# Chunk products of a delta-rule mixer spread over the four quarters of TensorE's array, with an upper-triangular solve reordered, in a two-layer decoder trunk

## The chip, the cores and the metric

The kernel runs on one core of one Trainium2 chip. The metric is the device time of one execution in microseconds (us). Three runs of the kernel before are shown; their median is 1519.89 us, from 1516.77 to 1520.2 us.

## What is computed

Two layers of a decoder trunk on 512 tokens of 1024 channels, all in fp32: a first layer whose mixer is half a gated linear recurrence (Griffin) and half an RWKV-7 time mix, a second layer whose mixer is retention, and after each mixer an MLP with squared ReLU. What the change touches is the recurrence of the RWKV-7 time mix, for 8 heads of 64 channels:

```python
def step(s, inp):
    r_t, w_t, k_t, v_t, z_t, bb_t = inp
    sz = jnp.einsum("bhij,bhj->bhi", s, z_t)
    s = s * w_t[:, :, None, :] + sz[..., None] * bb_t[:, :, None, :] + v_t[..., None] * k_t[:, :, None, :]
    return s, jnp.einsum("bhij,bhj->bhi", s, r_t)
...
_, y = lax.scan(step, s0, (tm(r_h), tm(w_h), tm(k_h), tm(v_h), tm(z_h), tm(b_h)))
```

Run token by token this would be 512 dependent steps. The kernel cuts the tokens into 8 chunks of 64 and does all that lies within a chunk by 64x64 matrix products, so that only 8 steps from chunk to chunk depend on each other.

## The kernel before, in words

The 8 heads go in 4 pairs (`PAIRS`), two heads of 64 channels over the 128 partitions. For each pair p the program runs `front_*` (projections of the pair, its vectors, and the normalising and output projection of pair p-1) and then `chunks_*`; after the last pair, `front_*` once more for the last output. Each engine has its own hand-written list of instructions (`_pe`, `_act`, `_dve`, `_pool`), and they meet only at semaphores: `need(...)` waits for names of this pair, `was(...)` for names of the pair before. After these stages come MLP, retention and MLP, which the change doesn't touch.

`chunks_pe` is the stage in question. A matrix of it is a tile of 128x512: partitions 0 to 63 hold one head, 64 to 127 the other, and every 64 columns are a chunk, so it holds 16 squares of 64x64. `by_chunk` (line 725) multiplies two such tiles square by square: 16 matmuls of 64x64 into one PSUM bank, each head's on its own rows and its own columns of the array. `ROWS` are the two halves of the partitions. There are 28 such products per pair. Four of them only turn a vector tile by multiplying with a unit matrix (`z_turned`, `v_turned`, `k_turned`, `b_turned`); the others make the chunk's triangular matrices (`azb`, `azk`, `ark`, `arb`), powers of the part on the 16-wide diagonal blocks (`m2`, `m4`, `m8`) and the inverse built from them (`e2`, `e4`, `e8` into `dt`), the rest of the inverse (`po`, `po2`, `sol`), and what the chunk-to-chunk steps need (`w1`, `w2`, `gg`, `qq`). Almost every result goes from PSUM to SBUF before it is used again, either by an ACT copy (`evac`, line 1002) or by a DVE operation (`masked` line 1196, `copied` 1200, `add` 1192, and line 1231).

```python
for c in range(NCH):
    cols = slice(c * C, (c + 1) * C)
    for rows in ROWS:
        mm = pe.matmul(bank[b][rows, cols], lhsT[rows, cols], rhs[rows, :] if rhs is eye2 else rhs[rows, cols],
                       start=True, stop=True)
```

The second part of `chunks_pe` is the loop over the 8 chunks (lines 902 to 919). For chunk c it first issues the products that need no state (902, 903 for the state, 907, 908 for the output), then waits for the state of the chunk before (`state`, a DVE multiplication at line 1238), adds the state's own product (915) into the same PSUM region, and the output's (919). `y_heads` ends it, and ACT's copy `ys` (938) and the next pair's `low_ranks` (783, 784) follow.

Weights stream through a ring of three buffers (`RING`): SP loads 1 MB, ACT rounds it (`split_hi`, 297), DVE takes the rest (`split_lo`, 303, 2.28 us for a full one), and PE waits in `chunk_ready`. Some of these splits stand inside `chunks_act` and `chunks_dve`. The pairs 1 and 2 (`FILLED`) have done the linear recurrence's last steps (`lru_drive`, `lru_scan`, `ya_out`, `ya_low`) in the front; pairs 0 and 3 do them on DVE in the chunk stage.

## Time and profile before

| | |
|---|---|
| runs, median (lowest to highest) | 1519.89 us (1516.77 to 1520.2) |
| the profiled execution, its own time | 1520.04 us |
| its span, first to last instruction | 1518.3 us |
| PE, PEld busy | 1475.6, 1232.3 us |
| DVE, ACT, POOL busy | 831.6, 504.0, 73.5 us |
| granted TensorE clock, mean | 0.986 |
| `by_chunk` matmul records, 4 pairs | 3584 |

The profiled execution lies 0.15 us from the median of the runs. PE is a matmul row of the profile, PEld a weight load. An fp32 matmul leaves two records of each kind, so that one `by_chunk` product of 16 matmuls leaves 32. A row's duration is from its first instruction's start to its last one's end; matmuls are pipelined, so the time from the start of one group to the start of the next is the rate.

### The profile page before, as it was taken

What the parts mean: (1) busy time and instruction counts of PE and PEld (TensorE: products, weight loads), DVE (VectorE), ACT (ScalarE), POOL (GpSimd) and SP (SyncE); (2) the same over time, 40 slices, a digit from 0 to 9 for tenths busy, and PEclk for the clock granted to TensorE, in tenths of its full rate; (3) what the DMA queues carried; (4) which work ended last, traced back from release to release, by engine and by line L of the source; (5) the groups of instructions that cost most, each with busy time, mean ns of one, the idle gap of its engine ahead of it and who ended that gap; (6) DMA issues with size and microseconds to landing.
All of it is one profiled execution on the core that took longest, in us unless ns stands there. A gap on an engine that the chain in (4) does not pass through costs nothing.

```text
span 1518.3 us, 23219 instructions
## 1 busy us (share of the span) xinstructions
PE 1475.6 (97%) x10404; PEld 1232.3 (81%) x10404; DVE 831.6 (55%) x1035; ACT 504.0 (33%) x578; POOL 73.5 (5%) x67
## 2 busy tenths in 40 slices
PE   7999999998999999999899999999998999999998
PEld 5888878786888888888788888888887888888886
DVE  7767585757644445363675455454447635354455
ACT  7444443534322222122343332332434313122222
POOL 1000000002100000000300000000003000000000
PEclk9999999998999999999899999999998999999999
DMA  4202020201322222223032213132131332222322
GB/s 180 71 8 98 3 89 18 84 4 56 125 95 100 92 102 90 105 88 107 28 111 84 83 58 109 57 104 91 56 111 42 112 110 83 93 102 90 105 88 79
DMA packets 19731, 125.62 MB, mean 83 GB/s; under 512 B 2288, under 2 KB 2288, under 8 KB 5808
## 3 DMA queue, kind: packets, MB, share of 16 engines
q1 hardware_dynamic: 19088, 121.23, 23.3%
q0 software_dynamic: 544, 2.91, 0.6%
q8 instruction: 82, 1.34, 0.4%
q14 instruction: 17, 0.14, 0.0%
HBM read 122.03 MB, written 2.10 MB: 82 GB/s over the span
## 4 chain that ended last, share of the span: by engine, by line
PE 88%; DVE 5%; ACT 3%; DMA 1%; POOL 1%; issue 1%; SPq 0%; DVEq 0%; POOLq 0%
PE bank L330 19%; PE bank L336 18%; PE bank L333 18%; PE bank L725 7%; PE bank L534 4%; PE bank L531 4%; PE bank L535 4%; PE bank L1331 2%; PE bank L1334 2%; PE bank L1328 2%; PE bank L344 2%; DVE XL L423 1%; DMA raw<-weights 1%; ACT WH L297 1%; POOL h L462 1%
## 5 line engine op out<-in xcount | busy, mean ns | idle before, releaser
L330 PE MATMUL bank<-XH,WH 128*128 128x512 f32 x944 | 381.6, 404 | 24.6 <-DVE XL L423 12.6
L333 PE MATMUL bank<-XL,WH 128*128 128x512 f32 x944 | 372.0, 394 | 0.0
L336 PE MATMUL bank<-XH,WL 128*128 128x512 f32 x944 | 371.8, 394 | 0.0
L303 DVE TENSOR_TENSOR WL<-raw,WH 128x2048 fp32r<-128x2048 f32 (+1 forms) x111 | 249.8, 2251 | 175.6 <-ACT WH L297 175.5
L297 ACT ACTIVATE WH<-raw 128x2048 fp32r<-128x2048 f32 (+1 forms) x111 | 208.4, 1877 | 277.7 <-DMA raw<-weights 277.7
L330 PEld LDWEIGHTS bank<-XH,WH 128*128 128x128 f32 x944 | 180.3, 191 | 66.6 <-issue 28.7
L333 PEld LDWEIGHTS bank<-XL,WH 128*128 128x128 f32 x944 | 180.5, 191 | 38.7 <-issue 2.6
L336 PEld LDWEIGHTS bank<-XH,WL 128*128 128x128 f32 x944 | 179.9, 191 | 38.9
L647 ACT ACTIVATE AH<-relu 128x512 fp32r<-128x512 f32 x64 | 40.5, 633 | 249.7 <-DVE relu L672 249.7
L330 PE MATMUL bank<-AH,WH 128*128 128x512 f32 x256 | 99.7, 389 | 0.1
L672 DVE SCALAR_TENSOR_TENSOR relu<-bank,rB 128x512 f32<-128x512 f32 x64 | 44.1, 690 | 101.3 <-PE bank L336 101.3
L333 PE MATMUL bank<-AL,WH 128*128 128x512 f32 x256 | 99.6, 389 | 0.0
L531 PE MATMUL bank<-WH,AH 128*128 128x512 f32 x256 | 99.6, 389 | 0.0
L534 PE MATMUL bank<-WL,AH 128*128 128x512 f32 x256 | 99.6, 389 | 0.0
L336 PE MATMUL bank<-AH,WL 128*128 128x512 f32 x256 | 99.6, 389 | 0.0
L535 PE MATMUL bank<-WH,AL 128*128 128x512 f32 x256 | 99.6, 389 | 0.0
L494 DVE TENSOR_TENSOR f<-f,bank 128x512 f32<-128x512 f32 x64 | 43.3, 686 | 90.8 <-PE bank L336 90.6
L725 PE MATMUL bank<-W,W 64*64 64x64 f32 x1920 | 63.2, 219 | 4.1 <-DVE W L1192 3.8
L725 PEld LDWEIGHTS bank<-W,W 64*64 64x64 f32 x1920 | 59.5, 135 | 6.9 <-issue 6.3
L330 PEld LDWEIGHTS bank<-AH,WH 128*128 128x128 f32 x256 | 48.0, 188 | 10.4 <-DVE AL L679 0.5
L531 PEld LDWEIGHTS bank<-WH,AH 128*128 128x128 f32 x256 | 48.0, 188 | 10.0
L333 PEld LDWEIGHTS bank<-AL,WH 128*128 128x128 f32 x256 | 48.0, 188 | 10.0
(298 smaller groups left out, 2054.3 us busy)
## 6 DMA issues: line engine op xcount, KB each, us to landing
raw<-weights SPq DMA_DIRECT2D x107, 1024.0 KB, 4.8
raw<-weights SPq DMA_DIRECT2D x8, 512.0 KB, 5.0
h<-x_fm SPq DMA_DIRECT2D x4, 512.0 KB, 8.0
out_tm<-hT SPq DMA_DIRECT2D x8, 256.0 KB, 2.1
rc<-ret_const POOLq DMA_DIRECT2D x1, 1536.0 KB, 6.8
pp<-pairs POOLq DMA_DIRECT2D x4, 199.0 KB, 5.1
cst<-const SPq DMA_DIRECT2D x1, 577.0 KB, 11.9
gain_row<-last_gain POOLq DMA_DIRECT2D x1, 512.0 KB, 3.5
```

The costliest lines, as they stand in the source:

```text
L297: nc.scalar.activation(WH[i][:, :n], raw[i][:, :n], ACT.Copy).then_inc(S("w_hi"), 1)
L303: nc.vector.tensor_tensor(WL[i][:, :n], raw[i][:, :n], WH[i][:, :n], ALU.subtract).then_inc(S("w_lo"), 1)
L330: mm = pe.matmul(bank[b][:], wh, xh, start=(k == 0), stop=False)
L333: mm = pe.matmul(bank[b][:], wh, xl, start=False, stop=False)
L336: mm = pe.matmul(bank[b][:], wl, xh, start=False, stop=(k == len(xs) - 1))
L494: nc.vector.tensor_tensor(f[:, m, :], f[:, m, :], bank[b][:], ALU.add).then_inc(S(f"acc_free{b}"), 1)
L531: mm = pe.matmul(bank[b][:], AH[:, kt, tok], wh, start=(kt == 0), stop=False)
L534: pe.matmul(bank[b][:], AH[:, kt, tok], wl, start=False, stop=False)
L535: mm = pe.matmul(bank[b][:], AL[:, kt, tok], wh, start=False, stop=(kt == KT - 1))
L647: nc.scalar.activation(AH[:, j, :], relu[:, j % 2, :], ACT.Square).then_inc(S("a_hi"), 1)
L672: nc.vector.scalar_tensor_tensor(relu[:, j % 2, :], bank[b][:], 0.0, rB[:], ALU.max, ALU.mult).then_inc(S(f"acc_free{b}"), 1)
L725: mm = pe.matmul(bank[b][rows, cols], lhsT[rows, cols], rhs[rows, :] if rhs is eye2 else rhs[rows, cols], start=True, stop=True)
```

## The change

It rewrites the chunk stage on all engines. Nothing outside `chunks_*` changes but two things: the copy `ys` reads another layout, and `front_dve` of pair 1 has one more `split_lo`.

1. Two neighbouring PSUM banks become a "twin" (`bank[2 * pr + j]`). A product of kind `vectors_to_t` or `turned` reads head j from rows j of the array and writes the result of chunk (i, par) to partitions `ROWS[par]` of bank 2·pr+j: its 16 matmuls use all four combinations of row half and column half. The matrices change layout with each such product (head on the partitions, or chunk parity on them). `kept` and `vectors_to_n` stay on the two diagonal quarters as before.
2. `two_vectors_to_t` and `two_turned`: two products with the same left factor become 16 matmuls of 64x128, the right factors side by side (azb_t with arb_t, azk_t with ark_t, e2 with m4_t, yz with yx).
3. `by_token`: the four turns become four 128x128 transpositions each.
4. `sol_t` goes; instead of one matrix for the solution, `t1z`, `t1x` and `ip2` are formed. The chunk's own products are 26: 13 on four quarters, 4 doubled on four quarters, 5 on two quarters, 4 of transpositions.
5. In the loop over chunks, the products without state move into `over_tokens`; they sum over tokens, which now lie on rows `ROWS[par]`, while the state's products sum over channels on rows of each head. Both add into the same PSUM region, and PE waits for its own semaphore `over_tokens` between them.
6. DVE and ACT lists are reordered. For pairs 0 and 3 `split_lo(4p+4)` moves from the middle of `chunks_dve` to its end; for pair 0 `split_lo(5)` moves to the front of pair 1.

```diff
-        def by_chunk(pe, b, lhsT, rhs, signal, left=0):
...
+        CH = [(i, par, j) for i in range(NCH // 2) for par in range(2) for j in range(2)]
...
+        def two_sums(pr, j, par, i):
+            return bank[2 * pr + j][ROWS[par], :].rearrange("p (w x) -> p w x", w=2)[:, :, i * C:(i + 1) * C]
...
+        def two_turned(pe, pr, lhsT, rhs, signal):
+            for i, par, j in CH:
+                rows, cols = ROWS[j], square(par, i)
+                mm = pe.matmul(two_sums(pr, j, par, i), lhsT[rows, cols], rhs[rows, :, cols], start=True, stop=True)
+            mm.then_inc(S(signal), 1)
...
+        def by_token(pe, b, vector, signal):
+            for i in range(NCH // 2):
+                mm = pe.transpose(bank[b][:, i * P:(i + 1) * P], vector[:, i * P:(i + 1) * P], eye)
+            mm.then_inc(S(signal), 1)
...
+        def turned(pe, pr, lhsT, rhs, signal):
+            for i, par, j in CH:
+                rows, cols = ROWS[j], square(par, i)
+                mm = pe.matmul(bank[2 * pr + j][ROWS[par], i * C:(i + 1) * C], lhsT[rows, cols], rhs[rows, cols],
+                               start=True, stop=True)
+            mm.then_inc(S(signal), 1)
...
+            vectors_to_t(pe, 3, W[5], W[6], "azb", 1)
+            need("lru_i", "rd_ready")
+            two_vectors_to_t(pe, 2, W[6], z_r, "azb_t")
+            pe.wait_ge(S("acc_free1"), use.now(1))
+            vectors_to_n(pe, 1, W[6], W[5], "azb_n")
+            need("nn", "nt", "g_out", "lru_r")
+            turned(pe, 1, W[0], W[1], "m2")
+            need("o")
+            turned(pe, 3, W[1], W[0], "m2_t")
+            need("nt_n")
+            by_token(pe, 1, W[5], "z_turned")
+            need("m2_s", "m2_ts")
+            turned(pe, 1, W[10], W[9], "m4")
+            need("e1")
+            two_turned(pe, 3, W[9], unit_squared, "e2")
...
+            need("m8_i", "e4_s")
+            turned(pe, 1, W[9], W[5], "e8")
...
+            need("w1_s", "b_by_token")
+            turned(pe, 1, W[7], Bt, "gg")
+            turned(pe, 2, W[7], lax, "qq")
...
+            for c in range(1, NCH):
+                i, par = c // 2, c % 2
+                prev = slice((c - 1) * C, c * C)
+                pe.wait_ge(S("over_tokens"), NCH * p + c + 1)
+                pe.wait_ge(S("state"), (NCH - 1) * p + c)
...
+                if c < NCH - 1:
+                    pe.wait_ge(S("over_tokens"), NCH * p + c + 1)
+                    over_tokens(c + 1)
...
+            if p == 1:
+                split_lo(dve, 4 * p + 1)
             split_lo(dve, 4 * p + 2)
...
+            if p not in FILLED:
+                split_lo(dve, 4 * p + 4)
+            if p:
+                split_lo(dve, 4 * p + 5)
```

What this does to the instructions' order, at three places. First PE at the start of pair 0's chunk stage. Names are tiles with their numbers (W0 to W11 are work tiles; `z_r` holds z and the decayed r side by side, `unit_squared` the unit-added matrix beside m2's turned form); a trailing x16 counts equal instructions. Before:

```order
L725 MATMUL bank5<-W5_67,W6_68 64x64 x16
L725 MATMUL bank6<-W6_68,W5_67 64x64 x16
L725 MATMUL bank7<-cst,W5_67 64x64 x16
L725 MATMUL bank2<-cst,W2_64 64x64 x16
L725 MATMUL bank3<-W1_63,W0_62 64x64 x16
L725 MATMUL bank4<-W0_62,W1_63 64x64 x16
L725 MATMUL bank7<-W5_67,W7_69 64x64 x16
L725 MATMUL bank2<-Rd_88,W7_69 64x64 x16
```

Now (a twin is printed by its first bank, so bank0 is bank 1 here):

```order
L744 MATMUL bank6<-W6_66,z_r_72 64x64 x16
L758 MATMUL bank4<-z_r_72,W6_66 64x2x64 x16
L777 MATMUL bank0<-z_r_72,W6_66 64x64 x16
L783 MATMUL bank2<-W1_63,W0_62 64x64 x16
L783 MATMUL bank6<-W0_62,W1_63 64x64 x16
L771 MATMUL bank0<-cst,z_r_72 128x128 x4
L783 MATMUL bank2<-W9_69,unit_squared_71 64x64 x16
L764 MATMUL bank6<-unit_squared_71,W9_69 64x2x64 x16
```

The turns of z and v, which stood as the third and fourth product and gave DVE time for its masks, are now four transpositions further on; m2 stands as the fourth product.

Second, PE in the loop over chunks, one round of pair 0. Before:

```order
L915 MATMUL bank4<-W3_65,W11_73 64x64 x2
L919 MATMUL bank2<-W10_72,W3_65 64x64 x2
L902 MATMUL bank3<-W9_71,Bt_79 64x64
L903 MATMUL bank3<-Vt_81,Kt_80 64x64
L902 MATMUL bank3<-W9_71,Bt_79 64x64
L903 MATMUL bank3<-Vt_81,Kt_80 64x64
L907 MATMUL bank2<-ARB_82,W9_71 64x64
```

Now:

```order
L1011 MATMUL bank2<-W3_65,W11_70 64x64 x2
L1015 MATMUL bank6<-unit_squared_71,W3_65 64x64 x2
L989 MATMUL bank0<-W9_69,Bt_78 64x64
L990 MATMUL bank0<-Vt_80,Kt_79 64x64
L989 MATMUL bank0<-W9_69,Bt_78 64x64
L990 MATMUL bank0<-Vt_80,Kt_79 64x64
L996 MATMUL bank6<-lax_89,W9_69 64x64
```

The instructions and their order are the same; what is new is which rows of the array they use and the wait on PE's own `over_tokens` ahead of 1011.

Third, DVE at the end of the last pair's chunk stage and in the front after it. Before:

```order
L1238 TENSOR_SCALAR W_65<-bank,PC 128x64 x7
L303 TENSOR_TENSOR WL_57<-raw_56,WH_58 128x2048
L494 TENSOR_TENSOR f<-f,bank 128x512
L1067 SCALAR_TENSOR_TENSOR Vt<-bank,Zt 128x512
L494 TENSOR_TENSOR f<-f,bank 128x512 x2
```

Now (line 1352 is the state's multiplication, 312 the split, 503 the addition to f, 1179 the centring of y):

```order
L1352 TENSOR_SCALAR W_65<-bank,PC 128x64 x7
L312 TENSOR_TENSOR WL_54<-raw_53,WH_55 128x2048
L312 TENSOR_TENSOR WL_57<-raw_56,WH_58 128x2048
L503 TENSOR_TENSOR f<-f,bank 128x512
L1179 SCALAR_TENSOR_TENSOR Vt<-bank,z_x 128x512
```

A second split of weights stands between the last state and the centring of y.

## Rows read from the trace of the kernel before

**Rows 1.** The page: busy time by engine, and the chain by line

```profile
PE 1475.6 (97%) x10404; PEld 1232.3 (81%) x10404; DVE 831.6 (55%) x1035; ACT 504.0 (33%) x578; POOL 73.5 (5%) x67
...
PE 88%; DVE 5%; ACT 3%; DMA 1%; POOL 1%; issue 1%; SPq 0%; DVEq 0%; POOLq 0%
PE bank L330 19%; PE bank L336 18%; PE bank L333 18%; PE bank L725 7%; PE bank L534 4%; PE bank L531 4%; PE bank L535 4%; PE bank L1331 2%; PE bank L1334 2%; PE bank L1328 2%; PE bank L344 2%; DVE XL L423 1%; DMA raw<-weights 1%; ACT WH L297 1%; POOL h L462 1%
```

**Rows 2.** Busy time by stretch: the chunk products, then pair 0's loop

```profile
core 0: us, PE busy (x) PEld busy (x) DVE busy (x) ACT busy (x) POOL busy (x), PEclk, DMA share, GB/s
61.67:89.59 27.92, 26.97 (x897) 26.65 (x897) 17.46 (x23) 13.11 (x17) 2.54 (x2) 1.00 0.08 22
89.59:95.53 5.94, 5.75 (x180) 5.45 (x175) 2.90 (x9) 0.00 (x0) 0.00 (x0) 1.00 0.03 6
144.06:171.90 27.84, 26.89 (x897) 26.58 (x897) 13.84 (x18) 8.96 (x13) 2.53 (x2) 1.00 0.07 23
```

**Rows 3.** Timeline, PE (start, us, engine, line, operation, tiles, count)

```profile
25.48 0.60 PE L350 MATMUL bank<-cst,small 128*128 128x128 f32 x4
25.84 0.48 PE L330 MATMUL bank<-XH,WH 128*128 128x512 f32 x1
...
47.16 1.02 PE L830 MATMUL bank<-W,cst 128*128 128x512 f32 x2
48.02 1.02 PE L832 MATMUL bank<-gate_in,pp 128*128 128x512 f32 x2
...
104.38 1.09 PE L740 MATMUL bank<-cst,lninv 128*64 128x128 f32 x16
105.40 0.50 PE L330 MATMUL bank<-XH,WH 128*128 128x512 f32 x1
```

**Rows 4.** Timeline, PE and its weight loads at pair 0's first products

```profile
61.12 0.39 PE L333 MATMUL bank<-XL,WH 128*128 128x512 f32 x1
61.35 0.39 PE L336 MATMUL bank<-XH,WL 128*128 128x512 f32 x1
61.67 2.08 PE L725 MATMUL bank<-W,W 64*64 64x64 f32 x64
63.58 2.03 PE L725 MATMUL bank<-cst,W 64*64 64x64 f32 x64
...
61.66 0.14 PEld L725 LDWEIGHTS bank<-W,W 64*64 64x64 f32 x2 [0.35 <-issue]
```

**Rows 5.** Timeline, all engines, from sol_t to w1 and its copy

```profile
83.59 1.23 PE L725 MATMUL bank<-W,W 64*64 64x64 f32 x32
...
84.94 0.69 DVE L1192 TENSOR_TENSOR W<-W,bank 128x512 f32<-128x512 f32 x1 [0.54 <-PE bank L725]
...
85.78 2.08 PE L725 MATMUL bank<-W,W 64*64 64x64 f32 x64 [0.95 <-DVE W L1192]
86.96 0.60 ACT L1002 ACTIVATE W<-bank 128x512 f32<-128x512 f32 x1 [4.52 <-PE bank L725]
```

**Rows 6.** Timeline, DVE: at the stage's entry, pair 0, then pair 1

```profile
61.77 0.69 DVE L718 TENSOR_TENSOR Uag<-bank,rB 128x512 f32<-128x512 f32 x1 [3.60 <-PE bank L336]
62.50 0.69 DVE L1155 SCALAR_TENSOR_TENSOR Kt<-ARB,Kt 128x512 f32<-128x512 f32 x1
63.11 1.38 DVE L1196 TENSOR_TENSOR W<-bank,cst 128x512 f32<-128x512 f32 x2
64.41 0.68 DVE L1196 TENSOR_TENSOR O<-bank,cst 128x512 f32<-128x512 f32 x1
...
144.17 0.69 DVE L492 COPY f<-bank 128x512 f32<-128x512 f32 x1 [0.67 <-PE bank L336]
```

**Rows 7.** Timeline, pair 0's loop: PE, then DVE

```profile
90.92 0.33 PE L915 MATMUL bank<-W,W 64*64 64x64 f32 x4 [0.19 <-DVE W L1238]
...
91.17 0.33 PE L902 MATMUL bank<-W,Bt 64*64 64x64 f32 x4
...
91.64 0.33 PE L915 MATMUL bank<-W,W 64*64 64x64 f32 x4
...
89.89 0.69 DVE L1192 TENSOR_TENSOR W<-Rd,bank 128x512 f32<-128x512 f32 x1 [0.31 <-PE bank L725]
90.50 0.28 DVE L1238 TENSOR_SCALAR W<-bank,PC 128x64 f32<-128x64 f32 x1
```

**Rows 8.** Timeline around the last pair's end: DVE, then PE

```profile
332.27 2.28 DVE L303 TENSOR_TENSOR WL<-raw,WH 128x2048 fp32r<-128x2048 f32 x1
...
335.30 0.69 DVE L1067 SCALAR_TENSOR_TENSOR Vt<-bank,Zt 128x512 f32<-128x512 f32 x1
...
337.78 0.95 PE L733 MATMUL bank<-cst,ARK 128*128 128x2 f32 x8
```

**Rows 9.** Timeline, DVE in pair 1's front

```profile
112.13 0.69 DVE L718 TENSOR_TENSOR Ur<-bank,rB 128x512 f32<-128x512 f32 x1 [0.18 <-PE bank L336]
...
133.23 0.69 DVE L718 TENSOR_TENSOR Uag<-bank,rB 128x512 f32<-128x512 f32 x1 [3.61 <-PE bank L336]
```

More of the change, by code:

```diff
@@ new lines, in turned, with kept @@
+        def turned(pe, pr, lhsT, rhs, signal):
+            for i, par, j in CH:
+                rows, cols = ROWS[j], square(par, i)
+                mm = pe.matmul(bank[2 * pr + j][ROWS[par], i * C:(i + 1) * C], lhsT[rows, cols], rhs[rows, cols],
+                               start=True, stop=True)
+            mm.then_inc(S(signal), 1)
+        def kept(pe, b, lhsT, rhs, signal):
+            for i, par, j in CH:
+                rows, cols = ROWS[j], square(par, i)
+                mm = pe.matmul(bank[b][rows, cols], lhsT[rows, cols], rhs[rows, cols], start=True, stop=True)
+            mm.then_inc(S(signal), 1)
@@ new lines, in chunks_pe, with over_tokens @@
+            turned(pe, 2, W[7], lax, "qq")
+            need("w2_s", "k_by_token")
+            def over_tokens(c):
+                i, par = c // 2, c % 2
+                rows = ROWS[par]
+                for j in range(2):
+                    cols = square(j, i)
+                    if c < NCH - 1:
+                        to = bank[1 + par][ROWS[j], i * C:(i + 1) * C]
+                        pe.matmul(to, Bt[rows, cols], W[9][rows, cols], start=True, stop=False)
+                        mm = pe.matmul(to, Kt[rows, cols], Vt[rows, cols], start=False, stop=(c == 0))
+                if c == 0:
+                    mm.then_inc(S("state_full"), 1)
+                for j in range(2):
+                    cols = square(j, i)
+                    to = bank[6 + par][ROWS[j], i * C:(i + 1) * C]
+                    pe.matmul(to, W[9][rows, cols], lax[rows, cols], start=True, stop=False)
+                    mm = pe.matmul(to, Vt[rows, cols], ARK[rows, cols], start=False, stop=(c == 0))
+                mm.then_inc(S("over_tokens"), 1)
@@ L899, in chunks_pe @@
+            over_tokens(0)
+            need("g_s")
+            over_tokens(1)
+            need("q_s")
+            for c in range(1, NCH):
+                i, par = c // 2, c % 2
                 prev = slice((c - 1) * C, c * C)
+                pe.wait_ge(S("over_tokens"), NCH * p + c + 1)
+                pe.wait_ge(S("state"), (NCH - 1) * p + c)
                 if c < NCH - 1:
                     for rows in ROWS:
-                        pe.matmul(bank[3 + c % 2][rows, cols], Bt[rows, cols], W[9][rows, cols], start=True, stop=False)
@@ L1222, in chunks_dve @@
[L1222 to L1233 removed]
+            need("po2")
@@ L1249, in front_pool @@
+            pool.wait_ge(*nth("nt_n", p + 1))
+            nc.gpsimd.tensor_tensor(chunked(W[4]), chunked(W[4]), table(K_EYE2), ALU.add).then_inc(S("e1"), 1)
         def front_pool(pool, p):
```

276 lines of the change are left out of this document (138 added, 138 removed).

## The prediction

> **What bounds the kernel now.** I read the page first: PE is busy for 97% of the span and holds 88% of the chain that ended last; DVE is at 55%, ACT at 33% [rows 1]. The program is bound by PE nearly everywhere, so a change pays by what it takes from PE's path. `by_chunk` (L725) alone is 7% of that chain, some 105 us. The table by stretch shows the stage the same way: of the 27.92 us of pair 0's chunk products PE is busy 26.97, and pair 1's stretch is 27.84 us long; then comes the loop with 5.94 us [rows 2]. Four pairs make some 135 us in which the change can act.
>
> **What a product costs now.** Two products run from 61.67 to the next group at 63.58 [rows 4]; over the stage the spacing is 0.933 us for 32 records, 29 ns each (the last of a row's records still needs 0.22 us: 64 records, 2.08 us, are 1.86 + 0.22). What is that 29 ns? A full-width fp32 product of 512 columns takes 48.02 - 47.16 = 0.86 us for two records, 0.43 each [rows 3], so 64 columns should take 0.43/8 = 54 ns. The stage runs twice as fast: the two heads' diagonal quarters work at the same time. The spread at L740 tells of the other direction: 16 records of 128 columns, each 107 ns by the same scale, would take 1.72 us one by one and take 105.40 - 104.38 = 1.02 [rows 3]. There both matmuls use all 128 rows and differ in the column half. So row halves overlap and column halves overlap; both at once, with four quarters, stands nowhere in the trace.
>
> **The change, part by part.**
>
> *Products on four quarters.* 13 single ones. Bounds: 0.933 us (no denser than the trace shows) and half of it, 0.467, if four overlap as two do now. I take 0.467, since either direction alone is shown to overlap fully. The 4 doubled ones: 32 records of 107 to 110 ns over four quarters, 0.88 us; if only two overlap, 1.76.
>
> *The rest of PE's list.* 5 products stay on two quarters, 5 x 0.933 = 4.67. 4 turns of four 128x128 transpositions: L350 has the same four, 0.60 us less the 0.16 that its last one needs beyond its slot, 0.44 each [rows 3], 1.76. They leave the 64x64 shape eight times per pair: at 61.35 the next start would have come 0.23 us later, at 61.58, and came at 61.67, with PEld idle for 0.35 [rows 4]. I take 0.09 a switch, 0.72; bounds 0 and 0.35. Sum: 13 x 0.467 + 4 x 0.88 + 4.67 + 1.76 + 0.72 = 16.7 us, against 28 x 0.933 = 26.1 now.
>
> *What PE will wait for.* With PE faster, the path product, copy, product matters. Its pieces: sol_t's first record at 83.59, DVE at 84.94, w1 on PE at 85.78: after DVE's end (85.63) 0.15 us; PE's last record ends 0.05 to 0.12 before the copy starts [rows 5]. An ACT copy is 0.60 us long, a DVE one 0.69, and DVE starts the next 0.61 to 0.65 later (63.11 to 64.41 for two); I take 0.61 [rows 5, 6]. I wrote the four new lists down against each other with these durations. For pair 0 five waits remain: m2 waits 0.60 for nt (DVE is busy with L718 and L1155 until 63.11, 1.44 after the stage's start [rows 6]), m4 0.46 for DVE's copy of m2_t, e8 0.42 for e4's copy, gg 0.49 for w1's, the turn of z 0.14. PE ends at 18.8 us after the start. In pairs 1 and 2 DVE is free 0.7 after the start (144.17 + 0.69 [rows 6]) and PE ends at 18.3; pair 3 enters like pair 0. The same writing-out gives 27.56 for the kernel before, 0.36 less than the 27.92 measured, so I add 0.36: 19.15 and 18.65. Gain: 2 x (27.92 - 19.15) + 2 x (27.84 - 18.65) = 35.9 us.
>
> *The loop.* Now the state's path sets it: L915 at 90.92, again at 91.64, 0.72 a round [rows 7]; PE's 24 records would need 0.70, so both are near. After the change PE issues state and output products (8 records, 0.23), `over_tokens` (16 records on two column halves of one row half, 0.47), then waits until the last of these is complete (0.16 more) and for the semaphore (0.06 to 0.10): 0.94 a round. The state's path (0.72) hides under that. Six rounds x 0.2 = 1.2 a pair, **4.8 us lost** in four. Bounds: 0 (if the state's path covers it) and 0.4 a round, 10 us.
>
> *The splits of weights.* Each is 2.28 us on DVE. In pair 3 a second one now lies between the last state and `head_centred` (L1067) [rows 8]. Before: split at 332.27, centring at 335.30, its square on ACT, and PE's sums at 337.78 without a wait. Now two splits end 4.56 after 332.27, then L494 and L1067 (0.61 + 0.07 + 0.69), ACT 0.63 and 0.1: 6.7 after, where PE arrives 5.5 after. PE waits **1.1 us**, once. In pair 1's front a further split comes after `kkinv`; L718 at 112.13 had waited for PE and moves 2.2 later. Queued behind it are the mixes, the convolution and `split_lo(7)`; DVE idles 3.61 us before 133.23 [rows 9], which takes it up. Cost 0; without that cover, 2.2. Pair 0's own split now ends where the next one ended before; PE's k projection may wait 0.2. SP's loads move earlier with the stage and have nothing to wait for.
>
> *Sum.* 35.9 - 4.8 - 1.1 - 0.2 = 29.8 us. From the profiled execution's 1520.04 that is **1490.2 us**; its distance of 0.15 from the median of the runs is nothing beside this.
>
> **The rivals.**
>
> *A. Starts come no closer than now.* The densest stretch of the trace is 29 ns a matmul record, each with its weight load [rows 2, 4]; issue or weight loading may be what sets it, and four quarters then change nothing for 64 columns. The doubled products would still pay. All 22 products but the turns cost 0.933: PE's list 20.5 + 1.76 + 0.72 = 23.0, with 0.9 of waits and the 0.36 24.3, a gain of 3.6 x 4 = 14.4, less 6.1: **1511.7 us**. For it: two row halves at 54 ns give 27, close to 29, and any other limit near there would look the same. Against: L740's spacing, also twice the single rate, is at 64 ns, so that 29 fits the columns and no fixed floor is needed to explain either. The Trainium skill ("TensorE: Matmul & The Clock Gate", Part 1, on the 56 ns) has such a floor at about 25 ns from start to start, whatever the columns; by that a single product would be 0.80 and a doubled one stays 0.88, and the estimate would be 1505. No row here shows a floor.
>
> *B. The copies set the stage.* DVE gets 18 operations of the stage and ACT 15, now with four-dimensional patterns over two banks. At the 0.61 spacing DVE needs 11.0 us and in pair 0 another 3.0 for the recurrence: under PE's 16.7. If the patterns make each copy half as long again (0.92 and 0.74), the lists end 4.8 later in pair 0 and 3.7 in pair 1, 17 in all: **1507 us**. For it: no row shows such a pattern. Against: L1196 reads a broadcast table in three dimensions and is as long (0.68) as a plain L718 (0.69) [rows 6]. The skill ("TensorEngine Tiling (Array Packing)", PSUM Bottleneck) says that after a fourfold speedup the copies may become the bound; the rows don't show that here.
>
> *C. Column halves on the same row half don't overlap for 64-row tiles.* Then single ones stay 0.933 and doubled ones 1.76; PE's list is 25.6 + 0.72 and the stage 27.6, a gain of 0.3 a pair. In the loop `over_tokens` uses one row half only and takes 0.93 instead of 0.47: with six rounds 2.8 more a pair. Sum: -1.4 + 11.3 + 4.8 + 1.3 = 16.0: **1536 us**, slower. It decides as soon as four records of 64 columns take 0.11 us, and not 0.06. For it: one row half has to feed two different streams, which no row shows (in L740 both take the unit matrix). Against: in L740 two matmuls of different column halves do overlap.
>
> **How the numbers follow.** The forecast has 0.60, A 0.17, B 0.09, C 0.10; 0.04 is for the rest. The forecast's own range: switches free and the loop at its old rate give 1482; the loop at 0.4 a round, switches at 0.35 (8 us more) give 1503. A and B reach to 1512. To leave no more than 2 in 10 out, the range goes from 1484 to 1512; C is outside. Within 0.3% (1515.5 to 1524.6, about what a measurement of this kernel can tell from no change) lies only a mixture, A with a dearer loop, or C with half its overlap: 0.05. Faster 0.85, slower 0.10.
>
> **What would show it.** In the profile after: `turned` rows (L783) of 16 matmuls every 0.47 us when nothing is waited for (0.8 to 0.93 is A, over 0.93 for doubled ones, L758 and L764, is C); `over_tokens` groups with L1011 every 0.94 us; transpositions (L771) at 0.44; copies at 0.60 and 0.69 (B otherwise); the chunk products about 19 us long per pair, the loop 7 us; DVE's idle time in the stage shrinking to a few us; an idle stretch of about 1 us on PE ahead of the head sums after the last pair. PE's granted clock should stay at 2.4 GHz through the stage, 1.00 in the stretches now [rows 2]: should the waits bring it to the lower level, the forecast is wrong by more than its terms. The forecast is wrong in its main term if the four quarters give less than 6 us a pair.

## The result, and the profile after

| | before | changed |
|---|---|---|
| runs on one chip, median (lowest to highest) | 1519.18 us (1516.77 to 1520.2) | 1494.09 us (1493.28 to 1496.79) |
| ratio, 95% interval | 1 | 0.9849 (0.9835 to 0.9863) |
| the profiled execution, its span | 1518.3 us | 1495.0 us |
| PE, PEld records | 10404 each | 9700 each |

The change is faster by 25 us, where 29.8 were forecast; 1494.1 lies in the range, 3.9 us above the number. The page of the changed kernel answers to [rows 1]:

```profile
PE 1445.6 (97%) x9700; PEld 1194.6 (80%) x9700; DVE 831.3 (56%) x1039; ACT 509.9 (34%) x590; POOL 73.2 (5%) x67
...
q8 instruction: 77, 1.26, 0.3%
...
PE 89%; DVE 5%; ACT 3%; issue 1%; POOL 1%; DMA 1%; SPq 0%; DVEq 0%; ACTq 0%; POOLq 0%
```

PE is still the bound. The line in the middle is a DMA queue (packets, MB, share) that the prediction passed over. It brings instructions, 1.26 MB in 77 packets of 16 KB. The 19400 records of PE and PEld are 252 to a packet. It is taken up again below.

Busy time by stretch of the changed kernel: pair 0's chunk products and its loop, then the chunk products of pairs 1, 2 and 3. Columns as in [rows 2].

```profile
63.15:83.42 20.27, 18.71 (x722) 16.88 (x721) 14.94 (x23) 12.00 (x19) 2.52 (x2) 1.00 0.09 30
83.42:90.85 7.43, 6.86 (x185) 5.95 (x176) 3.23 (x10) 2.56 (x2) 0.00 (x0) 1.00 0.01 2
139.52:159.08 19.56, 18.59 (x721) 17.09 (x720) 13.31 (x19) 9.76 (x16) 2.51 (x2) 1.00 0.09 30
215.55:236.99 21.44, 18.68 (x721) 17.01 (x721) 13.57 (x19) 9.69 (x16) 2.49 (x2) 1.00 0.09 29
282.04:303.75 21.71, 18.91 (x721) 16.94 (x721) 14.89 (x23) 11.99 (x19) 2.51 (x2) 1.00 0.16 52
```

The four chunk stretches are 82.98 us together. Before they were 27.92, 27.84, 28.40 and 28.37, together 112.53: 29.55 us are gained, not 35.9. The four loops, first start to last start, are 7.42, 7.78, 7.31 and 7.31 where they were 5.79 each: 6.7 lost. Two things lie outside. Pair 0's stage starts at 63.15 and not at 61.67, since PE's granted clock was at 1.2 GHz for most of the 4 us in the row below (of the changed kernel, 0.57 for the mean), and what follows pair 3 is 1.84 us shorter. In that last part, up to PE's last record, the clock was at the lower level for 37.5 us before and for 34.1 us in the changed kernel; by half of the difference, an estimate, up to 1.7 of the 1.84 are the clock's and not the change's. -29.55 + 6.7 + 1.48 - 1.84 is -23.2; the spans differ by 23.3.

```profile
23.50:27.50 4.00, 4.00 (x14) 3.17 (x13) 0.78 (x1) 1.26 (x1) 0.00 (x0) 0.57 0.00 0
```

That early fall of the clock was in some profiled executions of the kernels below and not in others with the same program up to there. It belongs to the execution, not to the change; the other three runs of the changed kernel are 2 to 3.5 us shorter than the profiled one.

Timeline of the changed kernel, PE at pair 0's first products (as [rows 4]):

```profile
63.15 0.69 PE L744 MATMUL bank<-W,z_r 64*64 64x64 f32 x32
63.66 1.05 PE L758 MATMUL bank<-z_r,W 64*64 64x128 f32 x32
64.54 1.11 PE L777 MATMUL bank<-z_r,W 64*64 64x64 f32 x32
65.97 1.25 PE L783 MATMUL bank<-W,W 64*64 64x64 f32 x64 [0.32 <-DVE W L1306]
67.15 0.66 PE L771 MATMUL bank<-cst,z_r 128*128 128x128 f32 x4
68.12 0.69 PE L783 MATMUL bank<-W,unit_squared 64*64 64x64 f32 x32 [0.32 <-DVE unit_squared L1314]
68.61 1.08 PE L764 MATMUL bank<-unit_squared,W 64*64 64x128 f32 x32
69.48 1.08 PE L758 MATMUL bank<-z_r,W 64*64 64x128 f32 x32
```

A single product on four quarters takes 0.49 us to the next start (68.12 to 68.61; its row of 0.69 less the last record's 0.22 is 0.47), where one took 0.93. A doubled one takes 0.87 (68.61 to 69.48). The waits for DVE's mask and for its copy of m2_t are there. The copies have their old lengths: timeline of the changed kernel, one of ACT and one of DVE.

```profile
66.72 0.60 ACT L1101 ACTIVATE W<-bank 128x512 f32<-128x512 f32 x1 [1.39 <-PE bank L783]
...
67.28 0.69 DVE L1314 COPY unit_squared<-bank 128x512 f32<-128x512 f32 x1 [0.22 <-PE bank L783]
```

So A (no closer starts), B (longer copies) and C (column halves don't overlap) all fall by the rows that were to decide. What then stretches the stage? The same view for pair 3, where two products break in their middle:

```profile
287.51 0.86 PE L764 MATMUL bank<-unit_squared,W 64*64 64x128 f32 x22
289.07 0.48 PE L764 MATMUL bank<-unit_squared,W 64*64 64x128 f32 x9 [0.70 <-issue]
...
295.10 0.62 PE L764 MATMUL bank<-z_x,W 64*64 64x128 f32 x16
296.64 0.67 PE L764 MATMUL bank<-z_x,W 64*64 64x128 f32 x16 [0.92 <-issue]
```

Nothing is waited for between two matmuls of one product, and yet PE and its weight loads stand still. "issue" names no releaser. In start-to-start time the long gaps are 0.54 us in pair 0, 0.55 in pair 1, 1.34 and 1.04 in pair 2, 0.97 and 1.19 in pair 3. Pair 1's is the only one that costs next to nothing: it lies in w2's product, and the wait ahead of gg, 0.47 us in pair 0, is not there. Laid beside the instruction queue's packets, each gap ends 1.24 to 1.55 us after one of them has arrived:

```
pair   packet arrived   PE goes on
0      72.72            74.27
1      156.50           157.94
2      218.82           220.33
2      224.04           225.28
3      287.65           289.07
3      295.21           296.64
```

That gave **theory S**: PE's instructions come in blocks of 256, one in 3.4 us or more. A product has 64 of them (16 matmuls, two passes each, each with its load). Two-quarter products at 0.93 us use a block in 3.73 us, which the queue keeps up with (the kernel before has one such stop, 0.47 us from start to start at 305.23, in pair 3); four-quarter ones at 0.47 us use it in 1.9. The Trainium skill ("Runtime: NRT & Kernel Launch", Instruction fetch mechanics) has the queue, the 16 KiB block of 256 instructions and that the next block is fetched while the current one runs; the trace agrees. It also says that this is hidden. The rows above say that here it is not.

The traces hold a sharper sign of S than the packets. Count every instruction of PE from the program's start, the matmul records, the weight loads and the few semaphore instructions among them, and divide by 256. In the traces of the two kernels and of the twelve experiments below there are 94 places inside a product of 64x64 tiles where PE stood idle for over 0.15 us and the profile names no releaser. All 94 have the remainder 193 or 194, whatever the product, the pair or the kernel; waits and tiles would spread them over all 256 remainders. What the stops share is their place in the count.

### The profile page after: what moved, and what is told of

Same layout as the page of the kernel before. It is cut to its first block, busy times and chain, and to the rows that moved or that the text cites. A ratio compares the mean times of both kernels' runs of the same rounds, so it can differ in the third digit from the quotient of the medians.

```text
span 1495.0 us, 21859 instructions
## 1 busy us (share of the span) xinstructions
PE 1445.6 (97%) x9700; PEld 1194.6 (80%) x9700; DVE 831.3 (56%) x1039; ACT 509.9 (34%) x590; POOL 73.2 (5%) x67
## 3 DMA queue, kind: packets, MB, share of 16 engines
q8 instruction: 77, 1.26, 0.3%
## 4 chain that ended last, share of the span: by engine, by line
PE 89%; DVE 5%; ACT 3%; issue 1%; POOL 1%; DMA 1%; SPq 0%; DVEq 0%; ACTq 0%; POOLq 0%
PE bank L339 20%; PE bank L345 20%; PE bank L342 19%; PE bank L543 4%; PE bank L540 4%; PE bank L544 4%; PE bank L1450 2%; PE bank L1447 2%; PE bank L1444 2%; PE bank L783 2%; PE bank L353 1%; PE bank L790 1%; DVE WL L312 1%; DVE XL L432 1%; POOL h L471 1%
## 5 line engine op out<-in xcount | busy, mean ns | idle before, releaser
L544 PEld LDWEIGHTS bank<-WH,AL 128*128 128x128 f32 x256 | 48.1, 188 | 10.0
L345 PEld LDWEIGHTS bank<-AH,WL 128*128 128x128 f32 x256 | 48.0, 188 | 9.9
```

Of the source, the lines that this page charges most:

```text
L345: mm = pe.matmul(bank[b][:], wl, xh, start=False, stop=(k == len(xs) - 1))
L544: mm = pe.matmul(bank[b][:], AL[:, kt, tok], wh, start=False, stop=(kt == KT - 1))
```

## The experiments

Theories beside S: **O**, the gaps belong to the stage's own order and waits; **F**, a least distance from start to start; **W**, the loop is set by PE's wait for its own `over_tokens`.

**1. The products without state two chunks ahead.** Three banks for the state and four for the output, so that `over_tokens(c + 2)` is issued where `over_tokens(c + 1)` was, and no wait for PE's own products is needed.

```diff
-                if c < NCH - 1:
-                    pe.wait_ge(S("over_tokens"), NCH * p + c + 1)
-                    over_tokens(c + 1)
+                if c < NCH - 2:
+                    over_tokens(c + 2)
```

> The products without state are issued two chunks ahead (chunk c+2 after the state's product of c), with three PSUM banks for the states and four for the outputs, so that PE's wait for its own over_tokens is met long before; the copy ys becomes three copies. Theory W (PE's wait for its own completion is what made a round 0.97 to 1.02 us in the changed kernel, against 0.72 before): rounds fall to 0.72 to 0.75, 1.5 us a pair; the longer copy at the end and the later third group give back some 0.6, so about 1490.5 us. Rival B (a round is dear because of the row halves that over_tokens uses: two column halves on one row half don't overlap fully): rounds stay near 1.0 and the time is 1494 to 1497.

Ratio 0.9831 (0.9816 to 0.9845), 1492.04 us. Timeline of this kernel, PE in pair 0's loop (L1015 is the state's product, L1011 in the changed kernel):

```profile
84.18 0.33 PE L1015 MATMUL bank<-W,W 64*64 64x64 f32 x4
...
85.78 0.33 PE L1015 MATMUL bank<-W,W 64*64 64x64 f32 x4
```

Two rounds in 1.60, 0.80 a round, where the changed kernel has 0.97 and 1.02 in turn; 0.72 to 0.75 had been expected. The four loops are 6.58, 6.63, 6.79 and 6.55 us: 3.3 less. In the changed kernel the wait is visible too (instructions of L1011, what ended PE's idle time before them):

```profile
L1011 PE MATMUL bank<-W,W x96: 218/228/267, 84.8 to 310.3; 64*64 64x64 f32 x96
...
  PE bank L997: 3.9, 20
```

W holds for 3.3 of the 6.7 us lost. Of the rest some 2 us (0.08 a round, 24 rounds) are that a round's 24 records on the new layout need 0.80 and not 0.72. That is not rival B: four neighbouring records still start in 0.12 us, and what is added lies where the next state product follows on `over_tokens` (0.20 in its place). By the totals alone the two kernels are not apart (the intervals overlap); by the rounds they are.

**2. Without doubling.** Each doubled product as two single ones, 256 instructions more a pair, the same columns.

```diff
-            for i, par, j in CH:
...
-                mm = pe.matmul(two_sums(pr, j, par, i), lhsT[rows, cols], rhs[rows, :, cols], start=True, stop=True)
+            for w in range(2):
+                for i, par, j in CH:
...
+                    mm = pe.matmul(two_sums(pr, j, par, i)[:, w, :], lhsT[rows, cols], rhs[rows, w, cols], start=True,
+                                   stop=True)
```

> Each of the 4 doubled products becomes two single ones of 16 matmuls with 64 columns, on the same four quarters, with the same left factors: PE gets 256 more instructions per pair (64 x 4) and nearly the same array time (0.93 for 0.88 us). Theory O (array time and waits for copies explain the stage): 0.2 us a pair, 1495 us. Theory S (PE's instructions come in 16 KB blocks of 256, and on four quarters it uses them up faster than the next block is ready, some 3.5 us each): up to 3.5 us more a pair, 1500 to 1508 us, with idle stretches of 0.5 to 1.5 us inside products that begin shortly after a block's packet has ended.

Ratio 0.9957 (0.9943 to 0.9971). The chunk stretches of this kernel, columns as before:

```profile
61.67:84.67 23.00, 19.39 (x850) 17.57 (x849) 15.04 (x23) 12.05 (x19) 2.52 (x2) 1.00 0.10 27
140.83:164.92 24.09, 20.66 (x850) 18.86 (x849) 13.32 (x19) 9.84 (x16) 2.50 (x2) 0.93 0.08 25
```

All four are 96.5 us, 13.5 more than in the changed kernel. Pair 0 has the clock at 1.00 throughout and is longer by 2.7 us, for 256 instructions at the same array time. In pairs 1, 2 and 3 the clock fell as well (0.93 each, 0.07 of 24 us, 1.7 us a pair at most): 5.1 of the 13.5. The other 8.4 are S's, 2.1 a pair, less than the 3.4 of a full block. In pair 0 the stops account for all of it: 0.68, 1.57 and 0.94 us, 2.65 more than the changed kernel's 0.54. The total, 1512.6 us by the ratio, is longer than the 1500 to 1508 that S had said, by about what the clock took, which S had not.

**3 and 4. The order of the 16 matmuls.** The same matmuls, in another order: one quarter after the other, and one column half after the other.

```diff
-        CH = [(i, par, j) for i in range(NCH // 2) for par in range(2) for j in range(2)]
+        CH = [(i, par, j) for j in range(2) for par in range(2) for i in range(NCH // 2)]
```

```diff
-        CH = [(i, par, j) for i in range(NCH // 2) for par in range(2) for j in range(2)]
+        CH = [(i, par, j) for par in range(2) for i in range(NCH // 2) for j in range(2)]
```

> The same matmuls on the same quarters, but quarter by quarter: four neighbours in the list use one quarter, then four the next. If each quarter has a queue deep enough for its four (16 instructions), a product still takes 0.47 us and the time is 1494. If PE looks only a few instructions ahead, the quarters work one after the other: a single product then takes 32 x 0.058 = 1.87 us and a doubled one 3.5, some 28 us a pair more, 1600 us. Anything between tells how far it looks.

> The order of the matmuls keeps to one column half for eight neighbours (both row halves in turn), then the other. This prices the use of four quarters at once. If only what stands next to each other overlaps, single products take 0.93 us and doubled ones 1.76, and the stage is 27.6 us a pair, as in rival C of the prediction: 1494 + 4 x 6.8 = 1521 us. With a deep look-ahead it stays at 1494.

Ratios 1.0227 (1.0212 to 1.0242) and 0.9896 (0.9881 to 0.9911). Pair 0's chunk stretch and, from the timeline, m2 with m2_t (two single products), first by quarter:

```profile
61.50:96.30 34.80, 34.26 (x716) 33.07 (x716) 15.82 (x23) 13.42 (x20) 2.53 (x2) 1.00 0.05 18
```

```profile
66.42 2.46 PE L783 MATMUL bank<-W,W 64*64 64x64 f32 x61
```

The same two of the kernel by column half:

```profile
61.52:83.75 22.23, 21.56 (x715) 20.28 (x716) 14.97 (x23) 12.24 (x19) 2.50 (x2) 1.00 0.09 28
```

```profile
64.54 1.56 PE L783 MATMUL bank<-W,W 64*64 64x64 f32 x64
```

61 records in 2.24 us are 37 ns each, against 15 in the changed kernel. The 37 ns lie between these 15 and the 54 of one quarter alone, the estimate of the prediction. So the quarters work fully side by side only where neighbours in the program lie on different ones; four successive matmuls on one quarter let the fifth overtake them only in part. Both totals, 1553.7 and 1503.4 us by the ratios, lie between the values that had been expected (1494 and 1600; 1494 and 1521). All four pairs by quarter take 34.83 us, alike to 0.01: a slow array has no gaps, as S says. By column half a single product takes 0.67 (64 records in 1.34), the stretches are 22.23 us in three pairs and 23.21 in the last, and only that one has a gap inside a product (0.48).

**5. The turns as fp32 products.** Two passes each, 32 instructions more a pair.

```diff
-                mm = pe.transpose(bank[b][:, i * P:(i + 1) * P], vector[:, i * P:(i + 1) * P], eye)
+                mm = pe.matmul(bank[b][:, i * P:(i + 1) * P], vector[:, i * P:(i + 1) * P], eye, start=True, stop=True)
```

> The four turns per pair are four matmuls with the unit matrix again, full 128 rows, instead of transpositions: the same 128 columns, but fp32 products leave two records each where a transposition leaves one. Theory S (PE's instruction supply, blocks of 256 instructions some 3.5 us apart, is what stretches the chunk stage of the changed kernel): each turn 0.44 us longer on the array (1.76 a pair, four turns) and 32 instructions more per pair (0.43 us of supply); 1499 to 1501 us, with a turn (L771) of 0.87 us from start to next start. Rival T (the turns lie under waits and cost nothing; their form is indifferent): 1493 to 1495.

Ratio 0.9893 (0.9872 to 0.9914), 1501.26 us. Timeline of this kernel, PE, z's turn in pair 1:

```profile
143.30 1.16 PE L771 MATMUL bank<-cst,z_r 128*128 128x128 f32 x8
144.39 0.69 PE L783 MATMUL bank<-W,unit_squared 64*64 64x64 f32 x32
```

A turn takes 1.09 to the next start; in the changed kernel z's takes 0.97 in pair 0, of which a wait of 0.32, which is gone here. The chunk stretches are 85.9 us, 2.9 more, not 7, and the loops are 1.2 longer: between T and S, since two turns lie under a wait (the idle time of 0.32 us behind z's and of 0.28 behind v's in the changed kernel are both gone here). By the ratio the kernel is 6.7 us slower, so only some 4 of it are found here, and I take nothing more from it.

**6. Half a block at the start.** 32 small matmuls (128 instructions) ahead of all; the stage is untouched.

```diff
+            for _ in range(32):
+                pe.matmul(bank[7][0:C, 0:C], vec[0:C, 0:C], vec[0:C, 0:C], start=True, stop=True)
```

> 32 small fp32 matmuls (64 columns, 128 instructions, half a block of 256) are issued once at the program's start into a bank that nobody reads; the chunk stage is that of the changed kernel, instruction for instruction. Theory S: the ends of the blocks fall at other places of the stage, so the long gaps move: the chunk products of the four pairs are no longer 20.3, 19.6, 21.4, 21.7 us but another set between 19.3 and 22, in which at least two pairs differ by over 0.5 us from before, and the gaps stand at other products; the total stays within 2.5 us of 1494. Rival O (the gaps belong to the stage's own order, tiles and waits): the same four durations to 0.2 us, gaps at the same products; the total 1494 to 1495.

Ratio 0.9872 (0.9854 to 0.9891). Chunk stretches of this kernel:

```profile
61.45:84.36 22.91, 19.04 (x722) 17.07 (x723) 14.94 (x23) 12.00 (x19) 2.51 (x2) 1.00 0.08 27
140.37:162.47 22.10, 19.23 (x722) 17.06 (x722) 13.79 (x19) 9.88 (x16) 2.51 (x2) 1.00 0.09 27
218.39:238.58 20.19, 18.77 (x721) 16.88 (x721) 13.48 (x19) 9.57 (x16) 2.50 (x2) 1.00 0.09 30
283.70:303.14 19.44, 18.26 (x721) 16.67 (x721) 14.83 (x23) 12.12 (x19) 2.51 (x2) 1.00 0.18 59
```

The same instructions take 22.9, 22.1, 20.2, 19.4 us, not 20.3, 19.6, 21.4, 21.7. Pair 3 has lost both long gaps, pair 0 has three (0.77, 1.05, 1.53). O falls. S's sizes were too narrow: two stretches are over 22 us, and by the ratio the kernel is 3.5 us slower than the changed one, not 2.5 at most.

**7. A whole block at the start.** The same with 64 matmuls.

```diff
+            for _ in range(64):
+                pe.matmul(bank[7][0:C, 0:C], vec[0:C, 0:C], vec[0:C, 0:C], start=True, stop=True)
```

> 64 small fp32 matmuls at the program's start, 256 instructions: a whole block, where the earlier run had half a one. Theory S: the ends of the blocks come back to where they are in the changed kernel, and with them the gaps: chunk products of about 20.3, 19.6, 21.4, 21.7 us (each within 0.5 us, since the arrival of a block also varies by itself), with the long gaps inside e2's product and inside yz's in pair 3; total 1494 to 1499 us (the small matmuls themselves cost what they did in the run with 32, up to 4 us). Rival V (the lengths vary from run to run and the number of instructions has no part in it): another set of lengths, as different from the changed kernel's as that of the run with 32.

Ratio 0.9877 (0.986 to 0.9893). First and last chunk stretch of this kernel:

```profile
66.63:87.18 20.55, 18.84 (x722) 17.06 (x722) 14.82 (x23) 11.99 (x19) 2.51 (x2) 1.00 0.10 30
...
285.48:306.67 21.19, 18.90 (x721) 16.93 (x721) 14.89 (x23) 11.98 (x19) 2.51 (x2) 1.00 0.15 53
```

20.55, 19.72, 20.50, 21.19: the changed kernel's set again, pair 2 a little outside the half microsecond (0.94). The gaps of pair 3 stand in e2's and yz's products, 6.1 and 13.2 us after its start (6.1 and 13.4 in the changed kernel). The place is set by the number of instructions ahead, the size also by when the block happens to arrive. The total, 1500.5 us by the ratio, lies 1.5 above the expected range. Experiments 1 and 11 have as many instructions ahead of pair 3 as the changed kernel, and their gaps stand in the same two products there (0.70 and 1.19 us; 0.98 and 1.19). V falls.

**8. The supply by itself.** 16 more products ahead of azb in pairs 1, 2 and 3, which nobody waits for.

```diff
+            for _ in range(16 if p else 0):
+                for i, par, j in CH:
+                    rows, c0 = ROWS[j], (2 * i + par) * C
+                    n = {1: C, 2: 16, 3: C}[p]
+                    out = bank[6 + j][ROWS[j if p == 3 else par], i * C:i * C + n]
+                    pe.matmul(out, W[5][rows, c0:c0 + C], W[6][rows, c0:c0 + n], start=True, stop=True)
```

> Ahead of azb, in pairs 1, 2 and 3, stand 16 more products of 16 matmuls each (1024 instructions, four blocks of 256), with nothing to wait for and nobody waiting for them. Pair 1: 64 columns on four quarters, the form of azb itself. Pair 2: the same with 16 columns. Pair 3: 64 columns on the two diagonal quarters. Theory S (the supply of instructions, a block of 256 every 3.4 us): pairs 1 and 2 take alike, 10 to 14 us, whatever the columns, in dense bursts with gaps of over 0.3 us between them; pair 3 takes the array's own 16 x 0.933 = 15 us with no gap. Rival F (a least distance from start to start of 25 to 27 ns a record): pairs 1 and 2 take 13 to 14 us at an even pace, with no gap. Rival R (no such limit; the gaps of the chunk stage come from its waits): pair 1 takes 16 x 0.467 = 7.5 us, pair 2 less than that. The whole kernel is longer by about the sum of the three stretches, less 1 to 2 us of waits that they cover.

This kernel was run once; all that is read from it lies within that one trace. Its timeline, PE: four quarters with 64 columns, four quarters with 16, two quarters with 64. L744 is azb, where each stream ends.

```profile
139.41 4.19 PE L935 MATMUL bank<-W,z_r 64*64 64x64 f32 x270
144.75 2.10 PE L935 MATMUL bank<-W,z_r 64*64 64x64 f32 x128 [1.15 <-issue]
148.75 1.90 PE L935 MATMUL bank<-W,z_r 64*64 64x64 f32 x113 [1.91 <-issue]
150.44 0.23 PE L744 MATMUL bank<-W,z_r 64*64 64x64 f32 x3
...
235.91 2.51 PE L935 MATMUL bank<-W,z_r 64*64 64x16 f32 x157
239.69 2.05 PE L935 MATMUL bank<-W,z_r 64*64 64x16 f32 x128 [1.27 <-issue]
243.69 6.58 PE L935 MATMUL bank<-W,z_r 64*64 64x16 f32 x226 [1.95 <-issue]
250.01 0.35 PE L744 MATMUL bank<-W,z_r 64*64 64x64 f32 x2
...
317.63 15.08 PE L935 MATMUL bank<-W,z_r 64*64 64x64 f32 x509
332.50 0.27 PE L744 MATMUL bank<-W,z_r 64*64 64x64 f32 x1
```

The first 270 records (540 instructions, two blocks and a little) run at 14.7 ns each, then PE stands for 1.15 us. Then come 128 records, which with their 128 loads are exactly a block, and again a gap. From block to block it is 4.00 us (144.75 to 148.75; 239.69 to 243.69). With 16 columns the gaps are the same and so is the pace inside a block, 14.4 to 14.7 ns. The stream on two quarters takes 14.87 us with no gap, 29 ns a record. S holds; F and R fall. Two points went otherwise. A starved block takes 4.0 us and not 3.4, although a stream that uses one in 3.72 us is not starved at all. And in pair 2 the granted clock fell from 2.4 to 1.2 GHz during the stream, in the second gap, so that its 14.1 us can't be set against pair 1's 11.03. A starved stream is thus slower per product (4.00/4 = 1.0 us) than one on two quarters (0.93). In an unbroken stream four quarters pay only for the two blocks or so that lie ready.

**9 and 10. 64 instructions less, first product.** t1z and t1x, with one left factor, as one doubled product on two quarters; the copies take half of both each. Alone, and on top of experiment 1.

```diff
-            kept(pe, 7, W[4], W[10], "t1z")
...
-            kept(pe, 2, W[4], W[11], "t1x")
+            for i, par, j in CH:
+                rows, cols = ROWS[j], square(par, i)
+                mm = pe.matmul(two_sums_kept(j, par, i), W[4][rows, cols], yzx[rows, :, cols], start=True, stop=True)
```

> t1z and t1x have the same left factor and become one doubled product on the two diagonal quarters, 16 matmuls of 64x128 in place of 32 of 64x64; the two copies each take half of both results. Array time is the same (2 x 0.93 against 1.87), 64 instructions less per pair. Theory S: up to 0.9 us less per pair, 1490 to 1493 us, most of it in the pairs with long gaps. Rival O: only the order of the copies changes; w1 now waits for the whole doubled product and its copy, 0.3 to 0.6 us more per pair: 1495 to 1497 us.

> Both edits together: the products without state two chunks ahead in the loop (measured alone: rounds of 0.80 us, ratio 0.9831), and t1z with t1x as one doubled product. If the doubled product gives what theory S says, 1488 to 1491 us; if it gives nothing, 1492, as with the loop's edit alone; if w1's longer wait decides, 1494.

Ratios 0.9917 (0.9896 to 0.9937) and 0.9878 (0.9855 to 0.9901): by the ratios 10 us slower than the changed kernel, and 7 us slower than experiment 1 alone. This was missed on both sides. w1 waits some 0.5 us more, in every pair. Pairs 1 and 3 take 23.3 and 24.3 us, with gaps of up to 1.9, pairs 0 and 2 take 20.4 with one of 0.8 at most. And in pair 3's loop of experiment 9 the clock fell, so that a round takes 1.65 us (row of that kernel, columns as before):

```profile
307.40:318.40 11.00, 9.73 (x188) 8.41 (x180) 3.75 (x10) 2.60 (x2) 0.00 (x0) 0.66 0.01 4
```

**11. Pair 3's split of weights back in the middle of the stage.** DVE's part; `split_hi` moves likewise on ACT, to behind m2's copy.

```diff
-            if p in FILLED:
+            if p != 0:
                 split_lo(dve, 4 * p + 4)
-            else:
+            if p not in FILLED:
                 lru_drive(dve, p)
...
-            if p not in FILLED:
+            if p == 0:
                 split_lo(dve, 4 * p + 4)
```

> In pair 3 alone the first split of weights goes back from the end of the chunk stage to its middle, where it stood before the change, on ACT and on DVE. The prediction had charged its place at the end with 1.1 us. If that price is real, 1492.5 to 1493.5 us; if the idle time of PE ahead of the head sums only takes the place of idle time that comes a little later, no difference (1494 to 1495), though the idle row ahead of the head sums (0.63 us) is gone; if the split delays DVE's operations in the stage, up to 2 us more.

Ratio 0.9858 (0.9843 to 0.9872) against 0.9849 (0.9835 to 0.9863): no difference in the totals. Timeline of the changed kernel, DVE's two splits and PE's head sums after pair 3 ([rows 8] before):

```profile
310.72 4.48 DVE L312 TENSOR_TENSOR WL<-raw,WH 128x2048 fp32r<-128x2048 f32 x2
...
317.12 1.05 PE L813 MATMUL bank<-cst,ARK 128*128 128x2 f32 x8 [0.63 <-ACT ARK L1044]
```

Counted from pair 3's last record of the loop, the head sums come at 5.27 us before, 6.06 in the changed kernel and 5.27 here. The next sums of f (L353) come at 26.7, 27.6 and 26.7. Behind them the clock falls, at a different point and for a different time in each execution, so that later places of these three can't be set side by side. (In this kernel's profiled run it fell in pair 1's loop as well, 10.05 us instead of 7.78, and the mean clock of its four runs, 0.983 to 0.985, is below the 0.986 to 0.987 of the changed kernel's. So the totals don't settle the price either.) The kernels of experiments 3 and 6 have the changed kernel's place of the split and, by chance, a fall of the clock like this one's. Busy time by stretch from the loop's end to the 600th PE record behind it, first this kernel, then experiment 6, then experiment 3:

```profile
316.48:455.55 139.07, 132.87 (x605) 109.36 (x604) 83.63 (x96) 43.64 (x51) 15.18 (x11) 0.95 0.25 87
310.45:450.51 140.06, 133.22 (x604) 109.33 (x604) 85.52 (x97) 43.65 (x51) 15.18 (x11) 0.95 0.24 87
365.57:505.53 139.96, 133.12 (x604) 109.36 (x604) 85.55 (x97) 43.64 (x51) 15.17 (x11) 0.95 0.24 87
```

With the split in the middle PE reaches this record 0.9 to 1.0 us earlier. So the charge of 1.1 us looks real and lasting; that the total shows nothing of it is, as far as the traces tell, the clock's doing.

**12. 64 instructions less, last product.** gg and qq doubled, on top of experiment 1.

```diff
-            turned(pe, 1, W[7], Bt, "gg")
-            turned(pe, 2, W[7], lax, "qq")
+            two_turned(pe, 2, W[7], b_lax, "gq")
```

> On top of the products without state two chunks ahead, gg and qq (same left factor W7) become one doubled product of 16 matmuls of 64x128 on four quarters: 64 instructions less a pair at the same array time (0.88 against 0.94 us). The sum for g on DVE now starts 0.4 us later and the third group without state waits for both sums. Theory S (a block of 256 instructions takes 3.4 to 4.0 us to come): 64 instructions are 0.85 to 1.0 us of supply a pair, less 0.4 to 0.6 for the later sums: 1490 to 1492 us, ratio 0.981 to 0.983, chunk products of the four pairs together 79 to 81 us. Rival L (a gap comes where a block's end happens to fall; fewer instructions only move it, and the later sums are paid in full): ratio 0.984 to 0.986, the four chunk stretches together no shorter than 81.4 us.

Ratio 0.9866 (0.9845 to 0.9886), and the four stretches are 20.37, 21.45, 20.52 and 22.39 us, 84.7 together, against 81.4 in experiment 1. Rival L: to take out 64 instructions moves the places of the gaps, and that can cost more than the instructions save. S says where a gap can be; it doesn't follow that a shorter list is faster.

## Why the prediction was right or wrong

**The forecast's case came, 25 us instead of 29.8.** What bounds the kernel, the two-quarter rate of 0.933 us, and the view that the two directions of overlap multiply: all shown. In the two profiled executions the clock took 1.5 us of the gain ahead of pair 0's stage and gave up to 1.7 back behind pair 3, so that the two nearly cancel. 0.467 for a single product and 0.88 for a doubled one were measured as 0.47 to 0.49 and 0.87. The turns cost more than 0.44 + 0.18: the four steps around them in pair 1 give some 0.1 us more each.

**The term that was mis-sized is the chunk products, 35.9 forecast and 29.55 measured.** The step that failed is "Sum: 13 x 0.467 + 4 x 0.88 + 4.67 + 1.76 + 0.72 = 16.7 us" together with the short list of waits. It took the array's time for PE's time. The waits themselves were sized well: for m2, m4, e8 and gg 0.47 to 0.59 us from the last start to the next (an idle time of 0.32 in the two rows above), against 0.60, 0.46, 0.42 and 0.49. Not in the list was that PE must also be given its 1443 instructions a pair. The forecast has 2 x 19.15 + 2 x 18.65 = 75.6 us for the four stretches, and they are 82.98, 7.4 more. (It also took pairs 2 and 3 of the kernel before to be as long as 1 and 0; they are longer, 1.0 us together, which is why only 6.4 are missing from the gain.) Of the 7.4, 5.1 are the five gaps of pairs 0, 2 and 3 in the table above (0.54, 1.34, 1.04, 0.97, 1.19, each counted from start to start, with a few hundredths that belong to the matmuls). Another 0.65 lie in po2's product of pairs 0 and 1, which takes 1.26 and 1.25 us to the next start and not 0.93: PE stops there too, for 0.28 and 0.26 us from start to start, and both stops have the remainder 193. The other 1.6 fit the turns, some 0.1 us for each of 16.

The bound of the old kernel, seen again: it used a block every 3.73 us, at or just under what the queue delivers. So 29 ns was near a second limit, as rival A suspected. A had the wrong limit: not a distance between starts but a rate over 256 instructions, which two ready blocks hide at the start.

**The loop: 4.8 forecast, 6.7 measured**, for the reason given. The round is 0.97 to 1.02 and not 0.94, and the first one 0.99 to 1.39. Bounds of 0 to 10 held.

**Pair 3's splits: 1.1 forecast.** PE was late by 0.8 at the head sums and by 0.9 at the sums of f, and against executions with a like clock 0.9 to 1.0 is left 140 us later (experiment 11). The charge was sized rightly as far as the traces tell.

**Pair 1's further split** cost nothing, as forecast: from stage to stage both kernels take 48.7 us between pair 0's loop and pair 1's stage. **The clock** stayed at 1.00 in the stages of the changed kernel's profiled run, as forecast. What the forecast did not have is that it can fall in a kernel whose chunk stage hardly differs: it fell in experiments 2, 8, 9, 10 and 11, in the stage or in the loop behind it. In 11 that loop takes 10.05 us in place of 7.78, in 9 10.84 in place of 7.31 (1.0 of it a gap of S). What decides whether it falls is not shown here.

**Open:** what decides when the next block is asked for (arrivals are 3.4 to 6.3 us apart in starved stretches), and so why two lists that differ by 64 instructions differ by 3 us in their gaps.

Of the kernels here the one with the products without state two chunks ahead has the lowest ratio, 0.9831; its interval overlaps with the changed kernel's.

## What to carry to other kernels

When a change makes small matmuls denser, count instructions beside array time. A 64x64 fp32 product of 16 matmuls is 64 instructions, and a stream of them gets only a block of 256 in 3.4 to 4.0 us once the two blocks lying ready are used up. More columns per matmul (here 128 instead of 64) are what the queue rewards; more quarters are worth it in short bursts between slower work. Alternate the quarters matmul by matmul. And compare places behind a local wait only between executions whose clock fell alike: a fall between them can hide or feign a microsecond.

## What the runs showed of the hardware that was not expected

- Instructions come to PE in blocks of 256. Two blocks and a little passed without a gap; from then on a block took 4.00 us when nothing else was to do, and PE went on 1.26 to 1.59 us after a packet's arrival. All 94 stops without a releaser inside products, in 14 traces, stand at the same remainder (193 or 194) of PE's instruction count by 256.
- A matmul record on four quarters takes 14.4 to 14.8 ns on average, with 64 columns as with 16. With 64 columns on two quarters it is 29 ns. The Trainium skill ("TensorE: Matmul & The Clock Gate", Part 1) has a least distance of about 25 ns from start to start; on four quarters the records lie closer.
- Four matmuls in a row on one quarter cost most of the overlap with the others: 37 ns a record instead of 15.
- The place of an instruction in its block decides the time of a stage: the same 1443 instructions took 19.4 to 22.9 us at a clock of 1.00.
